# Expert pair 14's down products placed ahead of pair 15's gate products, with the last experts' gate and up matrices loaded in halves

## The chip, the cores and the metric

The kernel runs on one core of one Trainium2 chip. The metric is the device time of one launch in microseconds (us). The kernel before was timed in three runs: 791.98, 792.37 and 793.82 us, median 792.37 us.

## What is computed

One decoder layer: a mixer (a combined input projection, a convolution group, a state-space scan and an output projection) and then a mixture of 32 SwiGLU experts, of which each token uses two. The change touches only the experts. Cut to that part, the reference is:

```python
def hier_moe(h, ...):
    ...
    acc = jnp.zeros_like(t)
    for e in range(N_EXPERTS):
        hid = jax.nn.silu(t @ w_gate[e]) * (t @ w_up[e])
        acc = acc + combine[:, e:e + 1] * (hid @ w_down[e])
    return acc.reshape(shp)
...
    xp = xp + hier_moe(rmsnorm(xp, ln_ffn[l]), ...)
y_prompt = rmsnorm(xp, ln_final)
```

All is float32. There are 320 tokens of 1024 numbers. Each expert has three matrices (gate and up 1024 x 512, down 512 x 1024), 2048 KB each, so 96 matrices are read.

## The kernel before, in words

**Pairs of experts.** The experts are worked on in 16 pairs; pair i is experts 2i and 2i+1. Up to 64 tokens of each expert are gathered into 128 rows, 64 per expert. An expert's work on TensorE (PE) is made of these steps, all written out by hand in the order in which PE runs them:

- `tokens_T` (L1191, transposes at L1196): turns the gathered rows of a pair.
- `gate_up` (L1208, products at L1213 and L1214): the gate and the up product of one expert, side by side in the two halves of a bank. Each of the 8 steps over k reads one eighth of both matrices.
- ScalarE (ACT) then takes the silu of the gate half (`silu`, L1577, L1581), and VectorE (DVE) multiplies it with the up half (its loop at L2025, issued at L2029; the operation shows under the helper's line L1654).
- `hidden_T` (L1219, transposes at L1225): turns the pair's hidden rows when both experts have theirs; ACT copies them out of the bank (L1599).
- `expert_down` (L1250, products at L1236): the down product of one expert. It waits for that copy.
- `rows_back` (L1583, L1587) on ACT copies the two halves of a down product out of its bank.
- `combine_most` and `combine_rest` (L1274 and L1279, products at L1261): 10 and 2 products per pair that add the pair's rows onto the tokens' rows, which stay in five banks to the end. They wait for `rows_back` of both experts.

**Order on PE** (loop at L1287 to L1307). Pair i's stage is: gate of 2i; `combine_most` of pair i-2; gate of 2i+1; tokens of pair i+1; `combine_rest` of pair i-2; the two downs of pair i-1; `hidden_T` of pair i. So a pair's downs come a stage after its gates, and its combine two stages after. After the last stage come `combine_most` and `combine_rest` of pair 14, a register load of a token count (`value_load`, L1308), the down of expert 30, and the down of expert 31 in two halves (`down_half`, L1240, products at L1246), and the last combine with the closing norm.

**Order on ACT** (loop at L1591): for pair i the two silus, `rows_back` of both experts of pair i-1, and the copy of the hidden rows.

**Loads.** SyncE (SP) issues every matrix as one DMA, in the order in which PE reads them (`expert_units`, L61). The matrices live in 11 slots; matrix j takes the slot of matrix j-11, and SP waits until the product that read that one is done (L576 to L583), then issues (`load_expert`, L502, its DMA is L503). PE waits for a matrix in `expert_landed` (L427). Three early matrices (expert 1's down, expert 4's up, expert 5's gate) load in halves (`load_half`, L559, DMA at L561), and the first gate product has a wait in its middle (L1211) for the second half of its tokens.

**Banks.** The gate, token, down and hidden results take three banks in turn, in the order of `moe_jobs` (L181); `job_free` (L361) makes PE wait until the result three jobs ago has been read.

Of the kernel before, what the change touches and what calls it, by code (L numbers as in the profile page):

```python
# [47 lines left out]
NE, EG, NG = 32, 8, 4  # L48
# [7 lines left out]
UNIT = 4096  # L56
UNITS = ["ub0", "ua0", "ub1", "ua1", "x0", "x1", "x2", "z0", "z1", "o0", "o1", "o2", "o3"]
N_MIX = len(UNITS)


def expert_units():  # L61


    units = []
    for i in range(NE // 2):
        units += [(m, 2 * i + j) for j in range(2) for m in range(2)]
        if i:
            units += [(2, 2 * i - 2), (2, 2 * i - 1)]
    return units + [(2, NE - 2), (2, NE - 1)]


EXPERT = expert_units()
E_AT = {unit: j for j, unit in enumerate(EXPERT)}

# [106 lines left out]
def moe_jobs():  # L181

    tokens = lambda i: [("tokens", (i, h), "xgt", 2 * i + h + 1) for h in range(2)]
    down = lambda i: [("down", 2 * i + j, "yo", 2 * i + j + 1) for j in range(2)]
    jobs = tokens(0)
    for i in range(NE // 2):
        jobs += [("gate", 2 * i + j, "hid", 2 * i + j + 1) for j in range(2)]
        jobs += tokens(i + 1) if i + 1 < NE // 2 else []  # L190
        jobs += down(i - 1) if i else []
        jobs += [("hidden", i, "hidt", i + 1)]
    return jobs + down(NE // 2 - 1)

# [9 lines left out]
def build(nc, A, O):  # L204
    hn_dram = nc.dram_tensor("hn_scratch", (T, D), F32).ap()
    with ExitStack() as ctx:
# [5 lines left out]
        def S(name):  # L212
            if name not in sems:
                sems[name] = ctx.enter_context(nc.semaphore("s_" + name))
            return sems[name]
# [81 lines left out]

        h0 = [ring[:, (N_MIX + c // 4) % R, D * (c % 4):D * (c % 4) + D].rearrange("p (b n) -> p b n", b=NB)
              for c in range(NC)]
# [6 lines left out]
        xgt = zf[:, 0:D].rearrange("p (k s) -> p k s", k=KD)  # L306
# [3 lines left out]
        own_half = [slice(CAP * b, CAP * b + CAP) for b in range(2)]  # L310
# [28 lines left out]
        first = zf[:, 2048:2048 + 3 * P].rearrange("p (u s) -> p u s", u=3)  # L339
# [21 lines left out]
        def job_free(pe, kind, at):  # L361


            n = M[kind, at]
            if n >= 3:
                pe.wait_ge(S(MOE_JOBS[n - 3][2]), MOE_JOBS[n - 3][3])
            return bank[n % 3]
# [47 lines left out]
        def landed(eng, unit):  # L415
# [4 lines left out]

        mix_slot = [ring[:, (N_MIX + m) % R, :] for m in range(R)]
        e_slot = [xcx[:, 0:UNIT], mix_slot[2], mix_slot[0], mix_slot[3], rb[:, 0:UNIT], mix_slot[1], mix_slot[4],
                  mix_slot[5], ra[:, 0:UNIT], vy[:, D:D + UNIT], xv[:, 0:UNIT]]
        n_slot = len(e_slot)
        expert_in = [S(f"expert_in{s}") for s in range(n_slot)]

        def expert_landed(eng, m, e):  # L427


            j = E_AT[m, e]  # L430
            if j == n_slot - 2:
                eng.wait_ge(S("tenth_half"), 16)
            if j in (n_slot, n_slot + 1):
                eng.wait_ge(S("first_halves"), 32)
            eng.wait_ge(expert_in[j % n_slot], 16 * (j // n_slot + 1))
            return e_slot[j % n_slot]
# [14 lines left out]
        def _(sp_):  # L451
# [13 lines left out]
            def slot_free(n):  # L465

                if n >= R:
                    old = UNITS[n - R]
                    if old == "o3":
                        sp_.wait_ge(filled, J[("outs",)] + 1)  # L470
                    elif old[0] == "o":
                        sp_.wait_ge(S("wo_used"), int(old[1]) + 1)
                    else:
                        sp_.wait_ge(filled, J[last[old]] + 1)
# [27 lines left out]
            def load_expert(j):  # L502
                sp_.dma_start(e_slot[j % n_slot], expert_src(*EXPERT[j])).then_inc(expert_in[j % n_slot], 16)  # L503
# [5 lines left out]
            def load_states(half):  # L509
                slot_free(N_MIX + half)  # L510
                for c in range(4 * half, 4 * half + 4):
                    sp_.dma_start(h0[c], pair(A["state_ssm"], c)).then_inc(S(f"h0_in{half}"), 16)
# [22 lines left out]
            for c in range(NC):  # L535
                sp_.wait_ge(S("h0_new"), c + 1)
                sp_.dma_start(pair(O["new_ssm_sample"], c), h0[c]).then_inc(S(f"h0_out{c // 4}"), 16)
                if c == 1:
                    slot_free(N_MIX + 2)
                    load_expert(1)  # L540
# [3 lines left out]
                if c == 4:  # L544
                    slot_free(N_MIX + 3)
                    load_expert(3)
# [6 lines left out]
            for m in range(4, R):  # L553
                slot_free(N_MIX + m)
                load_expert(m + 2)
# [17 lines left out]
            sp_.wait_ge(S("gu_done"), 1)  # L573
            for j in (n_slot, n_slot + 1):
                load_half(j, 1, expert_in[j % n_slot])
            for j in range(n_slot + 2, len(EXPERT)):  # L576
                m, e = EXPERT[j - n_slot]

                if m < 2:
                    sp_.wait_ge(S("gu_done"), e + 1)  # L580
                else:
                    sp_.wait_ge(S("dn_done"), e + 1)
                load_expert(j)  # L583

            gain = A["ln_final"].rearrange("(a d) -> a d", a=1)
# [205 lines left out]
        def _(pe):  # L791
# [399 lines left out]
            def tokens_T(i, h):  # L1191


                to = job_free(pe, "tokens", (i, h))
                for k in range(4):
                    ins = pe.transpose(to[:, P * k:P * k + P], gat[:, 4 * h + k:D:KD], ident[:, :])  # L1196
                ins.then_inc(S("xg_T"), 1)
# [7 lines left out]

                pe.transpose(b_t[:, 0:P], ident[:, :], ident[:, :])

            def gate_up(to, x, wg, wu, first=False):  # L1208
                for k in range(KD):
                    st = dict(start=k == 0, stop=k == KD - 1)  # L1210
                    if first and k == 4:  # L1211
                        pe.wait_ge(S("xgt"), 2)
                    pe.matmul(to[0:CAP, :], x[:, k, :], wg[:, FE * k:FE * k + FE], **st)  # L1213
                    ins = pe.matmul(to[CAP:P, :], x[:, k, :], wu[:, FE * k:FE * k + FE], **st)  # L1214
                    if first and k == 3:
                        ins.then_inc(S("gu_half"), 1)
                return ins
# [56 lines left out]
            def combine_most(i):  # L1274
                pe.wait_ge(S("places"), i + 1)
                pe.wait_ge(S("yo"), 2 * i + 2)
                to_tokens(back[i % 2], yo_of, PARTS[:-1])

            def combine_rest(i):  # L1279
                to_tokens(back[i % 2], yo_of, PARTS[-1:]).then_inc(S("added"), 1)  # L1280
# [3 lines left out]
                tokens_T(0, h)  # L1284
            after_read(pe, "slots")

            for i in range(NE // 2):  # L1287
                for e in (2 * i, 2 * i + 1):
                    if i >= 2 and e % 2:
                        combine_most(i - 2)  # L1290
                    gate, up = expert_landed(pe, 0, e), expert_landed(pe, 1, e)
                    to = job_free(pe, "gate", e)
                    pe.wait_ge(S("xgt"), 2 * i + 2 if e else 1)
                    gate_up(to, xgt[:, :, own_half[e % 2]], gate, up, first=e == 0).then_inc(S("gu_done"), 1)
                more = i + 1 < NE // 2
                if more:
                    pe.wait_ge(S("gath"), 16 * (i + 2))
                    for h in range(2):
                        tokens_T(i + 1, h)
                if i >= 2:  # L1300
                    combine_rest(i - 2)
                if i:
                    expert_down(2 * i - 2)
                    expert_down(2 * i - 1)
                hidden_T(i)
            combine_most(NE // 2 - 2)
            combine_rest(NE // 2 - 2)  # L1307
            over = pe.value_load(mcount[0:1, 0:1], min_val=0, max_val=T)  # L1308
            expert_down(NE - 2)
            w_down = expert_landed(pe, 2, NE - 1)  # L1310
# [36 lines left out]
        def _(act):  # L1347
# [229 lines left out]
            def silu(e):  # L1577
                b = e % 2
                act.wait_ge(S("gu_done"), e + 1)
                wait(act, S("hid"), e - 1)  # L1580
                act.activation(sil[b], job_bank("gate", e)[0:CAP, :], ACT.Silu).then_inc(S("sil"), 1)  # L1581

            def rows_back(e):  # L1583
                act.wait_ge(S("dn_done"), e + 1)
                pt = job_bank("down", e)
                for q in range(2):
                    ins = act.activation(yo[own_half[e % 2], 512 * q:512 * q + 512],  # L1587
                                         pt[CAP * q:CAP * q + CAP, :], ACT.Copy)
                ins.then_inc(S("yo"), 1)

            for i in range(NE // 2):  # L1591
                silu(2 * i)
                silu(2 * i + 1)
                if i:
                    rows_back(2 * i - 2)
                    rows_back(2 * i - 1)
                act.wait_ge(S("hid_T"), i + 1)
                wait(act, S("dn_done"), 2 * i)
                act.activation(hidt, job_bank("hidden", i)[:, :].rearrange("p (k s) -> p k s", k=4), ACT.Copy)\  # L1599
                    .then_inc(S("hidt"), 1)  # L1600
# [521 lines left out]
```

## Time and profile before

| | us |
|---|---|
| three runs | 791.98, 792.37, 793.82 |
| median of the runs | 792.37 |
| the profiled execution, its span from the first to the last instruction | 789.4 |
| median less span (what lies around the span) | 2.97 |
| PE busy in the span | 757.8 (96%) |
| mean rate of the DMAs in the span | 316 GB/s |

A time of the profiled execution beside its span is not recorded apart, so its span is what sums are made against. In rows of the trace, PE is TensorE, SPq is the queue on which SP issues DMAs, and "issue" in the chain is time in which PE waited for nothing that the profile shows; a wait for a matrix that is still landing shows like that here. A group of rows shows "us from the span's start" first.

### The profile page before, as it was taken

Reading aid. Unit: us, or ns where it says so; the run is one execution under the profiler, and the core shown is the slowest. Engines: PE = TensorE matmul, PEld = TensorE weight load, DVE = VectorE, ACT = ScalarE, POOL = GpSimd, SP = SyncE. Lnnn points to the kernel's source line nnn. Section 1 sums busy time; section 2 is a strip of 40 time slices with the busy share of each in tenths; the row PEclk is TensorE's granted clock in tenths of the full one; section 3 lists DMA queues with packets and bytes.
Section 4 is the critical chain, followed back from the end, with each engine's and each line's share of the span. In section 5 each row is a group of like instructions: output and inputs, shape, how many; then the busy total and the mean of one; then the engine's idle time right before and its main releaser. Section 6 shows DMA issues by size and latency. Waiting matters only on the chain.

```text
span 789.4 us, 8694 instructions
## 1 busy us (share of the span) xinstructions
PE 757.8 (96%) x3470; PEld 360.5 (46%) x3470; DVE 270.5 (34%) x629; ACT 154.4 (20%) x308; POOL 140.3 (18%) x168
## 2 busy tenths in 40 slices
PE   6999999999999999799999999999999999989896
PEld 4667677767843335434333333333333333333332
DVE  2399499985656423511101101110110011011003
ACT  3211121245712003202011112101111110110122
POOL 2279998612002000100000000000000000000000
PEclk9999999999999999799999999999999999999998
DMA  9990610042659786999999999999999999999982
GB/s 312 304 364 10 230 40 1 9 107 108 188 213 275 252 306 237 368 374 414 429 426 427 425 429 425 425 430 426 427 427 426 425 426 427 427 429 425 429 356 69
DMA packets 51400, 249.58 MB, mean 316 GB/s; under 512 B 6982, under 2 KB 24422, under 8 KB 38671
## 3 DMA queue, kind: packets, MB, share of 16 engines
q1 hardware_dynamic: 45460, 243.40, 77.2%
q10 hardware_dynamic: 3371, 2.81, 1.2%
q0 software_dynamic: 2528, 2.79, 1.1%
q8 instruction: 29, 0.48, 0.2%
q14 instruction: 12, 0.10, 0.0%
HBM read 246.87 MB, written 8.61 MB: 324 GB/s over the span
## 4 chain that ended last, share of the span: by engine, by line
PE 91%; DMA 3%; DVE 2%; SPq 2%; issue 2%; ACT 1%; POOLq 0%; DVEq 0%
PE bank L1213 28%; PE bank L810 18%; PE bank L1236 14%; PE bank L1076 9%; PE bank L1261 9%; DMA xcx<-in_state_conf_conv 2%; PE bank L1196 2%; SPq L491 1%; PE bank L1225 1%; PE bank L1065 1%; PE bank L1034 1%; PE bank L905 1%; PE bank L1214 1%; PE bank L1122 1%; PE bank L1047 0%
## 5 line engine op out<-in xcount | busy, mean ns | idle before, releaser
L810 PE MATMUL bank<-region_a,ring 128*128 128x320 f32 x576 | 157.2, 433 | 1.0 <-DMA ring<-in_w_in 1.0
L1654 DVE TENSOR_TENSOR region_a<-region_a,bank 64x512 f32<-64x512 f32 (+1 forms) x33 | 22.5, 680 | 377.6 <-ACT region_a L1581 377.6
L1214 PE MATMUL bank<-ring,zz 128*64 128x512 f32 x320 | 145.4, 610 | 0.0
L1213 PE MATMUL bank<-ring,zz 128*64 128x512 f32 x288 | 127.3, 595 | 2.7 <-issue 2.7
L810 PEld LDWEIGHTS bank<-region_a,ring 128*128 128x128 f32 x576 | 108.7, 190 | 46.3 <-DVE region_a L1654 1.1
L1655 DVE SCALAR_TENSOR_TENSOR bank<-region_a,par,bank 128x256 f32<-128x256 f32 x232 | 91.2, 479 | 0.0
L763 POOL DMA_INDIRECT region_a<-hn_scratch,region_a x16 | 15.9, 996 | 369.6 <-PE bank L1196 355.8
L1261 PE MATMUL bank<-zz,masks 128*128 128x512 f32 (+1 forms) x192 | 77.2, 603 | 0.7 <-ACT zz L1587 0.7
L1213 PEld LDWEIGHTS bank<-ring,zz 128*64 128x64 f32 x288 | 38.1, 137 | 82.5 <-issue 81.7
L1076 PE MATMUL bank<-ring,x_v_y 128*128 128x512 f32 (+1 forms) x192 | 74.0, 605 | 0.0
L1581 ACT ACTIVATE region_a<-bank 64x512 f32<-64x512 f32 x32 | 18.9, 590 | 271.5 <-PE bank L1214 271.5
L1587 ACT ACTIVATE zz<-bank 64x512 f32<-64x512 f32 x60 | 35.5, 591 | 106.7 <-PE bank L1236 106.3
L1236 PE MATMUL bank<-ring,xcx 128*64 128x512 f32 x240 | 53.8, 596 | 0.0
L1076 PEld LDWEIGHTS bank<-ring,x_v_y 128*128 128x128 f32 (+1 forms) x192 | 26.7, 171 | 43.3 <-issue 43.0
L1261 PEld LDWEIGHTS bank<-zz,masks 128*128 128x128 f32 (+1 forms) x192 | 26.6, 172 | 39.1 <-issue 39.1
L1214 PEld LDWEIGHTS bank<-ring,zz 128*64 128x64 f32 x320 | 43.4, 140 | 0.0
L674 POOL TENSOR_TENSOR x_v_y<-x_v_y 128x512 f32<-128x512 f32 x29 | 36.8, 1270 | 2.3
L1213 PE MATMUL bank<-x_v_y,zz 128*64 128x512 f32 x80 | 35.4, 595 | 0.5 <-issue 0.5
L1236 PEld LDWEIGHTS bank<-ring,xcx 128*64 128x64 f32 x240 | 16.5, 137 | 35.8 <-issue 35.8
L1213 PE MATMUL bank<-xcx,zz 128*64 128x512 f32 x64 | 30.8, 638 | 2.0 <-issue 2.0
L672 POOL TENSOR_TENSOR x_v_y<-region_a,par 128x512 f32<-128x512 f32 x30 | 32.2, 1074 | 2.2
L1214 PE MATMUL bank<-x_v_y,zz 128*64 128x512 f32 x64 | 28.3, 595 | 0.0
(313 smaller groups left out, 770.1 us busy)
## 6 DMA issues: line engine op xcount, KB each, us to landing
ring<-in_expert_w_up SPq DMA_DIRECT2D x20, 2048.0 KB, 24.4
ring<-in_expert_w_gate SPq DMA_DIRECT2D x17, 2048.0 KB, 30.3
ring<-in_expert_w_down SPq DMA_DIRECT2D x16, 2048.0 KB, 34.8
ring<-in_w_in SPq DMA_DIRECT2D x9, 2048.0 KB, 15.7
x_v_y<-in_expert_w_down SPq DMA_DIRECT2D x6, 2048.0 KB, 33.5
x_v_y<-in_expert_w_gate SPq DMA_DIRECT2D x5, 2048.0 KB, 34.6
ring<-in_w_out SPq DMA_DIRECT2D x4, 2048.0 KB, 10.0
xcx<-in_expert_w_gate SPq DMA_DIRECT2D x4, 2048.0 KB, 31.8
```

The costliest lines, as they stand in the source:

```text
L672: link(pool.tensor_tensor(tmp4, u_seq[:, :, :, k:k + TB], w4(par, k, NC), ALU.mult))
L674: return link(pool.tensor_tensor(acc, acc, tmp4, ALU.add))
L810: ins = pe.matmul(pt[0:m, 0:T], w[:, k, :], ht[:, k, :], start=k == 0, stop=k == KD - 1)
L1076: return pe.matmul(dst, mix, w, start=c == 0, stop=c == 2 * NC - 1)
L1213: pe.matmul(to[0:CAP, :], x[:, k, :], wg[:, FE * k:FE * k + FE], **st)
L1214: ins = pe.matmul(to[CAP:P, :], x[:, k, :], wu[:, FE * k:FE * k + FE], **st)
L1236: ins = pe.matmul(to[CAP * q:CAP * q + CAP, :], x[:, k, :], wd[:, D * k + 512 * q:D * k + 512 * q + 512], start=k == 0, stop=k == 3)
L1261: return pe.matmul(dst, rows[:, t0:t0 + n], of[q][0:rows.shape[0], :], start=False, stop=end)
L1581: act.activation(sil[b], job_bank("gate", e)[0:CAP, :], ACT.Silu).then_inc(S("sil"), 1)
L1587: ins = act.activation(yo[own_half[e % 2], 512 * q:512 * q + 512], pt[CAP * q:CAP * q + CAP, :], ACT.Copy)
L1654: tt_ = lambda out, a, b, op: dve.tensor_tensor(out, a, b, op)
L1655: stt = lambda out, a, s_, b, op0, op1: dve.scalar_tensor_tensor(out=out, in0=a, scalar=s_, in1=b, op0=op0, op1=op1)
```

## The change

Three things are done, all for the last pairs:

- The order on PE, on ACT, of the banks and of the matrices changes for pair 15: the downs of pair 14 come ahead of the gates of pair 15. PE now runs, after stage 14: the whole combine of pair 13, the downs of experts 28 and 29, the whole combine of pair 14, the gates of experts 30 and 31, `hidden_T` of pair 15, the register load, and the downs of 30 and 31 as before.
- ACT copies the down rows of experts 28 and 29 out ahead of the silus of 30 and 31.
- The gate and up matrices of experts 30 and 31 load in two halves each, in the order first half of gate, first half of up, second half of gate, second half of up. PE starts a gate product with the first halves and waits in its middle (k = 4) for the second.

```diff
--- before.py
+++ after.py
@@ -56,6 +56,7 @@
 UNIT = 4096
 UNITS = ["ub0", "ua0", "ub1", "ua1", "x0", "x1", "x2", "z0", "z1", "o0", "o1", "o2", "o3"]
 N_MIX = len(UNITS)
+LAST = NE // 2 - 1
 
 
 def expert_units():
@@ -63,9 +64,9 @@
 
     units = []
     for i in range(NE // 2):
-        units += [(m, 2 * i + j) for j in range(2) for m in range(2)]
-        if i:
-            units += [(2, 2 * i - 2), (2, 2 * i - 1)]
+        downs = [(2, 2 * i - 2), (2, 2 * i - 1)] if i else []
+        gates = [(m, 2 * i + j) for j in range(2) for m in range(2)]
+        units += downs + gates if i == LAST else gates + downs
     return units + [(2, NE - 2), (2, NE - 1)]
 
 
@@ -186,9 +187,10 @@
     down = lambda i: [("down", 2 * i + j, "yo", 2 * i + j + 1) for j in range(2)]
     jobs = tokens(0)
     for i in range(NE // 2):
+        jobs += down(i - 1) if i == LAST else []
         jobs += [("gate", 2 * i + j, "hid", 2 * i + j + 1) for j in range(2)]
-        jobs += tokens(i + 1) if i + 1 < NE // 2 else []
-        jobs += down(i - 1) if i else []
+        jobs += tokens(i + 1) if i < LAST else []
+        jobs += down(i - 1) if 0 < i < LAST else []
         jobs += [("hidden", i, "hidt", i + 1)]
     return jobs + down(NE // 2 - 1)
 
@@ -573,13 +575,22 @@
             sp_.wait_ge(S("gu_done"), 1)
             for j in (n_slot, n_slot + 1):
                 load_half(j, 1, expert_in[j % n_slot])
-            for j in range(n_slot + 2, len(EXPERT)):
+            def place_free(j):
                 m, e = EXPERT[j - n_slot]
-
-                if m < 2:
-                    sp_.wait_ge(S("gu_done"), e + 1)
-                else:
-                    sp_.wait_ge(S("dn_done"), e + 1)
+                sp_.wait_ge(S("gu_done") if m < 2 else S("dn_done"), e + 1)
+
+            for j in range(n_slot + 2, E_AT[0, NE - 2]):
+                place_free(j)
+                load_expert(j)
+            for e in (NE - 2, NE - 1):
+                pair_of = (E_AT[0, e], E_AT[1, e])
+                for j in pair_of:
+                    place_free(j)
+                    load_half(j, 0, S(f"late_half{e % 2}"))
+                for j in pair_of:
+                    load_half(j, 1, expert_in[j % n_slot])
+            for j in range(E_AT[2, NE - 2], len(EXPERT)):
+                place_free(j)
                 load_expert(j)
 
             gain = A["ln_final"].rearrange("(a d) -> a d", a=1)
@@ -1205,11 +1216,14 @@
 
                 pe.transpose(b_t[:, 0:P], ident[:, :], ident[:, :])
 
-            def gate_up(to, x, wg, wu, first=False):
+            def gate_up(to, x, wg, wu, first=False, late=None):
                 for k in range(KD):
                     st = dict(start=k == 0, stop=k == KD - 1)
                     if first and k == 4:
                         pe.wait_ge(S("xgt"), 2)
+                    if late is not None and k == 4:
+                        expert_landed(pe, 0, late)
+                        expert_landed(pe, 1, late)
                     pe.matmul(to[0:CAP, :], x[:, k, :], wg[:, FE * k:FE * k + FE], **st)
                     ins = pe.matmul(to[CAP:P, :], x[:, k, :], wu[:, FE * k:FE * k + FE], **st)
                     if first and k == 3:
@@ -1284,7 +1298,7 @@
                 tokens_T(0, h)
             after_read(pe, "slots")
 
-            for i in range(NE // 2):
+            for i in range(LAST):
                 for e in (2 * i, 2 * i + 1):
                     if i >= 2 and e % 2:
                         combine_most(i - 2)
@@ -1292,19 +1306,30 @@
                     to = job_free(pe, "gate", e)
                     pe.wait_ge(S("xgt"), 2 * i + 2 if e else 1)
                     gate_up(to, xgt[:, :, own_half[e % 2]], gate, up, first=e == 0).then_inc(S("gu_done"), 1)
-                more = i + 1 < NE // 2
-                if more:
-                    pe.wait_ge(S("gath"), 16 * (i + 2))
-                    for h in range(2):
-                        tokens_T(i + 1, h)
+                pe.wait_ge(S("gath"), 16 * (i + 2))
+                for h in range(2):
+                    tokens_T(i + 1, h)
                 if i >= 2:
                     combine_rest(i - 2)
                 if i:
                     expert_down(2 * i - 2)
                     expert_down(2 * i - 1)
                 hidden_T(i)
-            combine_most(NE // 2 - 2)
-            combine_rest(NE // 2 - 2)
+            combine_most(LAST - 2)
+            combine_rest(LAST - 2)
+            expert_down(NE - 4)
+            expert_down(NE - 3)
+            combine_most(LAST - 1)
+            combine_rest(LAST - 1)
+            for e in (NE - 2, NE - 1):
+
+
+                pe.wait_ge(S(f"late_half{e % 2}"), 32)
+                gate, up = (e_slot[E_AT[m, e] % n_slot] for m in range(2))
+                to = job_free(pe, "gate", e)
+                pe.wait_ge(S("xgt"), 2 * LAST + 2)
+                gate_up(to, xgt[:, :, own_half[e % 2]], gate, up, late=e).then_inc(S("gu_done"), 1)
+            hidden_T(LAST)
             over = pe.value_load(mcount[0:1, 0:1], min_val=0, max_val=T)
             expert_down(NE - 2)
             w_down = expert_landed(pe, 2, NE - 1)
@@ -1589,9 +1614,12 @@
                 ins.then_inc(S("yo"), 1)
 
             for i in range(NE // 2):
+                if i == LAST:
+                    rows_back(2 * i - 2)
+                    rows_back(2 * i - 1)
                 silu(2 * i)
                 silu(2 * i + 1)
-                if i:
+                if 0 < i < LAST:
                     rows_back(2 * i - 2)
                     rows_back(2 * i - 1)
                 act.wait_ge(S("hid_T"), i + 1)
```

## Rows read from the trace of the kernel before

**Rows 1.** The page's GB/s in 40 slices of the span.

```profile
GB/s 312 304 364 10 230 40 1 9 107 108 188 213 275 252 306 237 368 374 414 429 426 427 425 429 425 425 430 426 427 427 426 425 426 427 427 429 425 429 356 69
```

**Rows 2.** Chain of work that ended last, from 705 us: start, us, what.

```profile
705.67 2.69 issue
...
728.05 7.02 PE bank L1236 x32
735.07 0.68 PE bank L1225 x4
735.75 1.99 issue
...
746.42 3.63 PE bank L1261 x10
...
757.07 1.06 PE bank L1261 x2
758.13 7.04 PE bank L1236 x32
...
766.53 4.71 PE bank L1261 x12
771.24 3.58 PE bank L1236 x16
774.83 3.45 PE bank L1246 x32
```

**Rows 3.** SP's timeline: the issue of expert 30's up matrix.

```profile
696.07 0.33 SPq L503 DMA_DIRECT2D ring<-in_expert_w_up  x1
```

**Rows 4.** DMA issues of 696.0 to 696.3 us: KB, us from issue to landing.

```profile
ring<-in_expert_w_up SPq DMA_DIRECT2D x1, 2048.0 KB, 41.6
```

**Rows 5.** Line L503: down matrices into the ring; first and last start.

```profile
L503 SPq DMA_DIRECT2D ring<-in_expert_w_down x16: 327/328/3068, 348.2 to 726.1; - x16
```

**Rows 6.** DMA issues of 726 to 727 us: the last matrix, expert 31's down.

```profile
ring<-in_expert_w_down SPq DMA_DIRECT2D x1, 2048.0 KB, 41.3
```

**Rows 7.** Timeline of ACT after 757 us: silu, rows back, hidden copy, table load.

```profile
757.12 0.59 ACT L1581 ACTIVATE region_a<-bank 64x512 f32<-64x512 f32 x1 [10.07 <-PE bank L1214]
...
765.19 1.19 ACT L1587 ACTIVATE zz<-bank 64x512 f32<-64x512 f32 x2 [2.24 <-PE bank L1236]
766.41 0.60 ACT L1599 ACTIVATE xcx<-bank 128x512 f32<-128x512 f32 x1
767.02 1.28 ACT L1611 ACT_TABLE_LOAD   x1
```

**Rows 8.** Timeline of DVE: the product after the last silu.

```profile
757.74 0.69 DVE L1654 TENSOR_TENSOR region_a<-region_a,bank 64x512 f32<-64x512 f32 x1 [9.90 <-ACT region_a L1581]
```

**Rows 9.** SP's timeline near 341 us: second halves of two early matrices.

```profile
340.98 0.33 SPq L561 DMA_DIRECT2D xcx<-in_expert_w_up  x1
341.35 0.43 SPq L561 DMA_DIRECT2D ring<-in_expert_w_gate  x1
```

**Rows 10.** DMA issues of 341.3 to 341.6 us: those two halves, us to landing.

```profile
xcx<-in_expert_w_up SPq DMA_DIRECT2D x1, 1024.0 KB, 7.8
ring<-in_expert_w_gate SPq DMA_DIRECT2D x1, 1024.0 KB, 9.9
```

**Rows 11.** PE's timeline in the first gate product, about its middle.

```profile
336.90 0.59 PE L1213 MATMUL bank<-xcx,zz 128*64 128x512 f32 x1
337.33 0.59 PE L1213 MATMUL bank<-xcx,zz 128*64 128x512 f32 x1
```

**Rows 12.** PE's timeline: start of expert 24's gate product.

```profile
648.75 1.00 PE L1213 MATMUL bank<-region_b,zz 128*64 128x512 f32 x1 [1.90 <-issue]
```

**Rows 13.** Stretches: busy PE, PEld, DVE, ACT, POOL; then PEclk, DMA share, GB/s.

```profile
650.00:654.00 4.00, 4.00 (x16) 1.48 (x14) 0.00 (x0) 0.00 (x0) 0.00 (x0) 0.72 1.05 442
...
708.00:710.00 2.00, 1.64 (x8) 0.74 (x10) 0.00 (x0) 0.00 (x0) 0.00 (x0) 1.00 0.96 410
...
738.00:740.00 2.00, 2.00 (x6) 0.55 (x5) 0.00 (x0) 0.00 (x0) 0.00 (x0) 0.50 0.98 418
```

## The prediction

> **What bounds the kernel now.** I read the page's rates first. From about 340 us to 765 us the DMAs move 425 to 430 GB/s without a break, and only the last two slices fall off [rows 1]: in the expert stage the stream of matrices runs flat out. The chain of waits then shows how PE stands to that stream. PE is busy almost throughout, but at the start of a pair it waits for a matrix: 2.69 us ahead of expert 28's gate product and 1.99 us ahead of expert 30's [rows 2]. That these are landings is seen from SP: expert 30's up matrix was issued at 696.07 us [rows 3] and landed 41.6 us later [rows 4], at 737.67; the gate product starts at 735.75 + 1.99 = 737.74. The last matrix, expert 31's down, was issued at 726.1 [rows 5] and landed 41.3 us later [rows 6], at 767.4. Between the two landings lie six matrices, so one takes (767.4 - 737.67)/6 = 4.95 us. PE starts expert 31's down only at 774.83 [rows 2], 7.4 us after its landing. So up to 737.7 us the stream sets the pace, and from there PE alone does. What the end costs is PE's own work from there, and every hole in it.
>
> **What the change removes.** The next matrices in line become the downs of 28 and 29. They take the places that expert 30's gate and up had, so they land at 732.7 and 737.7, and PE has other work until then. The wait of 1.99 us is gone. A second loss goes with it. The gate product behind that wait took 746.42 - 737.74 = 8.68 us, expert 31's only 757.07 - 750.05 = 7.02 us (750.05 is the end of the ten combine products, 746.42 + 3.63) [rows 2]. The cause is the clock: granted clock 0.50 from 738 to 740 us [rows 13], which is the 1.2 GHz level. A fall thus costs 1.66 us. Both together are 3.65 us.
>
> **What it adds: PE's new order, step by step.** I start at 735.07, where the downs of 26 and 27 end and the transposes of pair 14's hidden rows begin [rows 2]; up to there nothing changes, since the order of the matrices is the same up to expert 27's down.
>
> 1. The combine of pair 13 needs the rows of expert 27 copied back. The same step stands in the trace one pair on: downs end at 758.13 + 7.04 = 765.17, ACT copies for 1.19 us [rows 7], the combine starts at 766.53 [rows 2]. That is 1.36 us, with the transposes inside it. So the combine starts at 736.43 and takes 4.71 as pair 14's does [rows 2]: 741.14.
> 2. Downs of 28 and 29, 7.04 us [rows 2]: 748.18. Their matrices have landed, and the hidden rows of pair 14 were copied long before.
> 3. Again 1.36 us until the rows of 29 are back: 749.54. Before, the transposes of pair 15 filled half of this hole; now nothing does.
> 4. Combine of pair 14, 4.71: 754.25.
> 5. Gates of 30 and 31, 7.02 each: 768.29.
> 6. Now the pair's hidden chain stands bare. Before, it lay behind the combine and the downs of pair 14. Its parts: gate end to product end 758.43 - 757.07 = 1.36 (silu, then DVE's product) [rows 7, 8]; transposes 0.68 [rows 2]; ACT's copy 0.60 [rows 7]; the three hand-overs between PE and ACT or DVE, 0.03, 0.05 and, as from ACT's copy to the combine, 766.53 - 766.38 = 0.15. Together 2.87: the down of 30 starts at 771.16.
>
> Before, it starts at 771.24 [rows 2]. From there on all is as before. **The sum is -0.08 us.** What is saved, 1.99 + 1.66, is given back as a bare hidden chain (2.87) and as longer holes at the two copies back.
>
> **What costs nothing, and what covers it.** The halves are eight DMAs of 1 MB in place of four of 2 MB, so four more issues on SP of 0.33 to 0.43 us each [rows 9], 1.7 us at most, while SP issues some 41 us ahead of a landing [rows 4, 6]. Two second halves in the trace were issued at 340.98 and 341.35 [rows 9] and landed 7.8 and 9.9 us later [rows 10], at 348.78 and 351.25: 2.47 us apart, half of a whole matrix's 4.95. So I take no loss of rate. Expert 31's second halves land at about 757.5; the product's middle is at 761.27 + 3.5 = 764.8. The cover is 7.3 us there, and as much for the last down (767.4 against 774.7). If it were gone, each us over it would be paid in full. The mid-product wait: in the first gate product, which has one, its ninth pair starts 0.43 us after its eighth [rows 11], the pace of the others, so a satisfied wait is free; the other end, from the same rows, is one lost pair per gate, 0.86 us in all, and I take 0. The register load on PE used to sit behind twelve combine products; now it sits behind four transposes, with 0.60 us of ACT's copy over it. On ACT the same load and its branch leave no gap: the copy ends at 767.01, the table load starts at 767.02 [rows 7], so it fits. Bound: 0 to 0.6, I take 0. SP's later waits (the final gain, the last downs) ask for the same products as before, and these end no later.
>
> The Trainium skill's page DMA: Bandwidth & Descriptors (Anatomy of one DMA — SWDGE (gpsimd) path) gives about 2 us of fixed cost for each DMA, on a path other than SP's. By it, as an estimate, four more would make the stream 8 us late, 0.7 us more than its cover; the landings 2.47 us apart speak against that here.
>
> **The unknown: the clock in the new stall.** A fall of the clock is the term that decides. The trace has three waits of such a length. After 1.90 us ahead of expert 24's gate [rows 12] the clock was 0.72 in the next stretch [rows 13]; after 1.99 us it was 0.50; after 2.69 us it stayed at 1.00 [rows 2, 13]. So two of three. The new hidden chain keeps PE from products for 2.87 us (2.19 us idle, the rest transposes), like those. I take a fall there as more likely than not, at 1.66 us, all on the path, since only downs and the last combine follow. A second place: a fall behind the 2.69 us wait did not happen in this execution. Before the change the wait of 1.99 us would have swallowed it; now nothing would, and it would be worth another 1.66. The three runs lie 1.84 us apart, about one fall, so I expect it to differ from run to run.
>
> **Forecast**, chance 0.40: one fall after the change, where the profiled execution had one: -0.08 + 1.66 = +1.58 us, 789.4 + 1.58 = 790.98 of span. The span lies 2.97 us under the median of the runs, which I leave as it is: 792.37 + 1.58, about 794.0 us.
>
> **Rivals.**
>
> - *No fall in the new stall* (0.22). For it: one of three stalls, and the transposes break it. Time 792.37 - 0.08 = 792.3. The Trainium skill's page TensorE: Matmul & The Clock Gate (Why this matters for your kernels) blames longer idle gaps than these for the clock's return to the low level; by it this rival would hold, but the fall after 1.90 us speaks against it.
> - *One fall more than that* (0.27): both places, or one place against runs of before that had none. For it: in two of three stalls the clock fell. +3.24: 795.6.
> - *Faster: the stream is the brake* (0.08). Before the change PE waits for expert 30's matrices in full; after it, it has 7 us in hand. If the six matrices up to there took 5.2 us each instead of 4.9 (735.75 + 1.99 less 705.67 + 2.69 is 29.4 for six), the old wait would be 1.8 us longer and the change worth -1.9: 790.5. It decides from 5.15 us on. Against it: 4.90 and 4.95 in two stretches of the trace.
> - *Halves do harm* (0.03): a fixed cost for each DMA, or SP's issues blocked. It needs over 7 us to show; at 8 us it gives +0.7, 793.1 without a fall and 794.7 with one.
>
> **How the numbers follow.** About 0.2%, 1.58 us, is what a measurement of this kernel can tell from no change; the forecast sits on that line. Slower by more: the 0.27, a little over half of the forecast's 0.40, and part of the last rival, 0.52. Same: the 0.22 and the rest of the forecast, 0.40. Faster: 0.08. The range goes from 791.2 (no fall, and a stream 1 us slower) to 796.0 (two falls and 0.4 of the bounds); it leaves out the faster rival and three falls.
>
> **What would show it.** In the profile after: no wait ahead of expert 30's gate; the combine of pair 13 some 1.4 us behind the downs of 27; a second such hole behind 29's; about 2.9 us between the last gate product and the first down product of 30, and the downs of 30 starting near 771 us where no fall preceded. The halves show as eight issues of 1024 KB, none of them waited for. Right on the clock is a granted clock of 0.50 behind the last gates. Wrong: a wait inside gates 30 or 31 (halves late), a hidden chain much shorter or longer than 2.9 us, or downs of 30 that start well before 770 us, for which I have no step.

## The result, and the profile after

The change made the kernel slower: 796.42 us median of 20 runs (793.46 to 799.0) against 793.5 us of the kernel before, also in 20 runs (790.55 to 797.9). The ratio is 1.0033, 95% interval 1.0018 to 1.0047, or 2.6 us of 793.5. It is not the quotient of the two medians, which lie 2.92 us apart. The direction and the larger share of the chances were right; the time of 794.0 us was too low, and 796.42 lies 0.4 us above the range.

The span of the profiled execution is 792.1 us, against 789.4. With the result each run's span stands beside its time: the two are 1.66 to 1.90 us apart in every run, not 2.97. So, as an estimate, the profiled execution before was a run of some 791.2 us, 2.3 us under the median of 20; the one after took 793.83 us, 2.6 us under its own. Both lie under their medians by about as much, so they can be set against each other.

The chain of waits after the change (start, us, what) answers to [rows 2]; first the wait ahead of expert 28's gate, then all from the downs of experts 26 and 27 on:

```profile
708.54 0.95 issue
...
729.17 7.04 PE bank L1250 x32
...
736.84 0.60 ACT zz L1612
737.44 0.14 issue
737.58 4.71 PE bank L1275 x12
742.28 7.04 PE bank L1250 x32
...
749.95 0.60 ACT zz L1612
750.55 0.14 issue
750.69 4.71 PE bank L1275 x12
755.39 0.57 PE bank L1227
...
768.85 0.42 PE bank L1227
...
769.33 0.60 ACT region_a L1606
...
769.95 0.70 DVE region_a L1682
770.65 0.14 issue
770.79 0.73 PE bank L1239 x4
...
771.54 0.61 ACT xcx L1627
772.15 0.09 issue
772.24 5.35 PE bank L1250 x16
777.59 3.45 PE bank L1260 x32
```

L1250 is a down product, L1275 the combine, L1227 a gate product, L1239 the transposes. The order is the predicted one. The downs of 26 and 27 end at 736.21, the combine of pair 13 starts 1.37 us later (1.36 was said), the second such hole is 1.37 us too, the two gates end at 769.30, and the hidden chain stands bare for 2.94 us (2.87 was said). From the end of those downs to the down of 30 it is 772.24 - 736.21 = 36.03 us; the prediction had 36.09, and the kernel before 36.17 [rows 2]. So in this stretch nothing was won.

What the profile lost lies at two other places. Expert 30's down took 5.35 us where the old one took 3.58 [rows 2]: 1.77 us for a fall of the clock. The stretches (busy PE, PEld, DVE, ACT, POOL; then granted clock, DMA share, GB/s) show it, beside the earlier fall that this execution had behind its wait of 3.09 us at the start of pair 13:

```profile
680.00:684.00 4.00, 4.00 (x14) 1.46 (x12) 0.00 (x0) 0.00 (x0) 0.00 (x0) 0.57 1.02 430
...
772.00:776.00 4.00, 3.76 (x10) 1.42 (x12) 0.00 (x0) 1.63 (x3) 0.00 (x0) 0.57 0.02 4
```

And the stretch began 1.14 us later (736.21 against 735.07), which no part of the change explains, since order and loads are the same up to there. It is there at the start of expert 26's gate already, 679.47 us against 678.30. Together -0.14 + 1.77 + 1.14 = 2.77, and the spans differ by 2.7.

Another distance is of use below. The last wait for a matrix in the change is the one of 0.95 us ahead of expert 28's gate, which starts at 709.49 us. From there on PE alone sets the pace, and the down of 30 follows 772.24 - 709.49 = 62.75 us later. In the kernel before it is 771.24 - 708.36 = 62.88 us, with a fall of the clock inside [rows 2].

The halves were on time but their issue was not as cheap as said. Part of SP's timeline (start, us, what; x2 is two issues with the time between them) and the landing of expert 31's last half (KB, us to landing):

```profile
708.11 6.75 SPq L563 DMA_DIRECT2D ring<-in_expert_w_up  x1
714.90 4.25 SPq L563 DMA_DIRECT2D region_b<-in_expert_w_gate  x1
719.20 4.23 SPq L563 DMA_DIRECT2D ring<-in_expert_w_up  x1
723.47 4.49 SPq L563 DMA_DIRECT2D region_b<-in_expert_w_gate  x1
728.00 4.24 SPq L563 DMA_DIRECT2D ring<-in_expert_w_up  x1
732.29 6.39 SPq L505 DMA_DIRECT2D ring<-in_expert_w_down  x2
```

```profile
ring<-in_expert_w_up SPq DMA_DIRECT2D x1, 1024.0 KB, 31.2
```

SP stood 4.2 us and more in each of these five issues of halves, not 0.33 to 0.43. PE did not wait for it: the last half landed at 728.0 + 31.2 = 759.2, and PE reached the middle of that product some 3.5 us ahead of its end at 769.30, at 765.8.

### The profile page after: what moved, and what is told of

It is laid out like the page before. It is cut to its first block, busy times and chain, and to the rows that moved or that the text cites. A ratio compares the mean times of both kernels' runs of the same rounds, so it can differ in the third digit from the quotient of the medians.

```text
span 792.1 us, 8698 instructions
## 1 busy us (share of the span) xinstructions
PE 761.2 (96%) x3470; PEld 362.9 (46%) x3470; DVE 272.7 (34%) x629; ACT 154.5 (20%) x308; POOL 140.2 (18%) x168
## 4 chain that ended last, share of the span: by engine, by line
PE 73%; DVE 5%; issue 2%; ACT 1%; DMA 0%; DVEq 0%; POOLq 0%
PE bank L1227 28%; PE bank L1250 14%; PE bank L1087 9%; PE bank L1275 9%; PE bank L1207 2%; PE bank L1239 1%; DVE bank L1683 1%; PE bank L821 1%; PE bank L1076 1%; PE bank L1045 1%; PE bank L916 1%; PE bank L1228 1%; DVE x_v_y L1683 1%; DVE bank L1721 1%; PE bank L1133 1%
## 5 line engine op out<-in xcount | busy, mean ns | idle before, releaser
L1228 PE MATMUL bank<-ring,zz 128*64 128x512 f32 x320 | 142.1, 599 | 0.0
L1227 PE MATMUL bank<-ring,zz 128*64 128x512 f32 x288 | 127.3, 595 | 0.9 <-issue 0.9
L1275 PE MATMUL bank<-zz,masks 128*128 128x512 f32 (+1 forms) x192 | 76.9, 602 | 2.1 <-ACT zz L1612 2.1
L1227 PEld LDWEIGHTS bank<-ring,zz 128*64 128x64 f32 x288 | 38.1, 137 | 80.7 <-issue 80.0
L1250 PE MATMUL bank<-ring,xcx 128*64 128x512 f32 x240 | 55.5, 611 | 0.7 <-ACT xcx L1627 0.7
L1275 PEld LDWEIGHTS bank<-zz,masks 128*128 128x128 f32 (+1 forms) x192 | 26.6, 172 | 40.4 <-issue 40.4
L1227 PE MATMUL bank<-x_v_y,zz 128*64 128x512 f32 x80 | 37.1, 618 | 3.1 <-issue 3.1
L1250 PEld LDWEIGHTS bank<-ring,xcx 128*64 128x64 f32 x240 | 17.2, 140 | 36.9 <-issue 36.9
L1227 PE MATMUL bank<-region_b,zz 128*64 128x512 f32 x64 | 28.2, 594 | 2.3 <-issue 1.7
L1228 PE MATMUL bank<-x_v_y,zz 128*64 128x512 f32 x64 | 28.3, 595 | 0.0
```

Of the source, the lines that this page charges most:

```text
L1250: ins = pe.matmul(to[CAP * q:CAP * q + CAP, :], x[:, k, :], wd[:, D * k + 512 * q:D * k + 512 * q + 512], start=k == 0, stop=k == 3)
L1275: return pe.matmul(dst, rows[:, t0:t0 + n], of[q][0:rows.shape[0], :], start=False, stop=end)
```

## The experiments

Every kernel was timed in 12 runs, beside 22 to 35 runs of the kernel before on the same chip. One interval is 0.0014 to 0.0022 wide on either side, some 1.1 to 1.7 us, so single microseconds are seen only as a pattern over several kernels, or as distances within the traces. The quotient of two medians differs from the ratio given by up to 0.0011.

### The two halves of the change apart

**The order alone.** The matrices of 30 and 31 load whole:

```diff
-            for j in range(n_slot + 2, E_AT[0, NE - 2]):
...
+            for j in range(n_slot + 2, len(EXPERT)):
                 place_free(j)
                 load_expert(j)
...
-                pe.wait_ge(S(f"late_half{e % 2}"), 32)
-                gate, up = (e_slot[E_AT[m, e] % n_slot] for m in range(2))
+                gate, up = expert_landed(pe, 0, e), expert_landed(pe, 1, e)
```

> The change's order without its halves: the gate and up matrices of experts 30 and 31 load whole. Theory (the bare hidden chain, the longer holes at the copies back and the clock's falls cost the time; the halves do nothing): same as the change, 1.0033 of before within about 0.0015, and in the profile no wait ahead of expert 30's gate, some 2.9 us between expert 31's last gate product and expert 30's first down product. Rival (the halves hold up the stream or SP): back to 0.999 to 1.001 of before, with matrices landing earlier than in the change's profile.

Measured: 795.97 us, ratio 1.0029 (1.0015 to 1.0043). No wait ahead of expert 30's gate. Its chain behind the last gate product:

```profile
773.88 0.60 ACT region_a L1593
...
775.20 0.14 issue
775.33 0.74 PE bank L1229 x4
...
776.70 0.09 issue
776.79 3.65 PE bank L1240 x16
```

The same bare chain, and here the clock did not fall: it was granted at 1.00 from 774 to 780 us, and the down took 3.65 us. From the start of expert 28's gate to the down of 30 it is 776.79 - 714.04 = 62.75 us, as in the change. So the order is what costs; a help or harm from the halves does not show within the intervals.

**The halves alone**, in the old order: SP and `gate_up` as in the change, the loops of PE, ACT and the banks as before.

```diff
-                    gate, up = expert_landed(pe, 0, e), expert_landed(pe, 1, e)
+                    late = e if e >= 30 else None
+                    if late is None:
+                        gate, up = expert_landed(pe, 0, e), expert_landed(pe, 1, e)
+                    else:
+                        pe.wait_ge(S(f"late_half{e}"), 32)
+                        gate, up = (e_slot[E_AT[m, e] % n_slot] for m in range(2))
...
```

> The old order with the change's halves: the gate and up matrices of experts 30 and 31 load in halves, PE starts with the first ones. Theory: expert 30's gate starts without its wait of about 2 us, since its first halves have landed at about 732.8 us of the old profile and the second ones land within the product; nothing is laid bare. Start of the down of 30 some 2.0 us earlier, and 1.7 us more in executions whose clock fell behind that wait: 0.9960 to 0.9980 of before. Rival (halves do harm): 1.000 or more, with a wait in the middle of a gate product.

Measured: 791.4 us, ratio 0.998 (0.9963 to 0.9996): faster than before. PE's timeline at expert 30's gate, and at the down of 29:

```profile
736.15 0.75 PE L1241 MATMUL bank<-ident,region_a 128*128 128x128 f32 x4
736.82 0.64 PE L1229 MATMUL bank<-xcx,zz 128*64 128x512 f32 x1
```

```profile
760.23 3.65 PE L1252 MATMUL bank<-ring,xcx 128*64 128x512 f32 x16 [1.03 <-DMA ring<-in_expert_w_down]
```

The gate starts right behind the transposes: the wait of 1.99 us [rows 2] is gone, and nothing was moved for it. Half of that comes back: PE now waits 1.03 us for the down of 29, which is the stream's next landing. So the halves took the old wait away by themselves, at the upper edge of the expected range, and the reordering spent more than that.

### The clock

**A first try, mis-sized.** The change with full-width products in the new stall, whose results nobody reads:

```diff
+            def warm(to, n):
+                for _ in range(n):
+                    pe.matmul(to[:, :].rearrange("p (a e) -> p a e", e=P), ident[:, :],
+                              bc(ident[:, :].unsqueeze(1), [P, 4, P]), start=True, stop=True)
...
+            warm(job_free(pe, "hidden", LAST), 3)
             hidden_T(LAST)
+            warm(job_free(pe, "down", NE - 2), 1)
```

> The change with three products whose results nobody reads ahead of the last transposes of hidden rows and one behind them, so that PE runs products while it waits for the hidden chain. The chain itself is as long as before. Theory (a fall of the clock in that stall is part of the loss): no granted clock of 0.50 on expert 30's down, which takes 3.6 us and not 5.35; the time lies 0.9 to 1.5 us under the change's: 1.0015 to 1.0022 of before. Rival (only the stall's length costs, the clock falls elsewhere as often): 1.0033 as the change.

Measured: 796.31 us, ratio 1.0037 (1.002 to 1.0053). The filling was too long. Each product shows as two of 0.46 us:

```profile
769.75 2.77 PE bank L1244 x6
...
773.85 3.58 PE bank L1255 x16
```

The stall grew from 2.94 to 4.10 us, by 1.16. That the ratio hardly rose hints that something was saved against it, but it settles nothing.

**The same with half-width products** (`to[:, 0:2 * P]`, 256 columns):

> The change with products whose results nobody reads in the new stall, this time half as wide (256 columns, 0.43 us each): three ahead of the last transposes, one behind them, 1.72 us in all, so that they fit into the stall of 2.97 us. Theory (falls of the clock in that stall are part of the loss): the down of 30 still starts about 2.97 us behind the last gate product, takes 3.58 us in every profile and no granted clock of 0.50 lies on it; time 1.0018 to 1.0026 of before. Rival (the clock's falls cost nothing on the mean): 1.0033.

Measured: 794.27 us, ratio 1.0017 (0.9998 to 1.0036).

```profile
770.60 1.49 PE bank L1244 x6
...
772.11 0.73 PE bank L1239 x4
...
772.86 0.60 ACT xcx L1634
773.47 0.09 issue
773.56 3.65 PE bank L1255 x16
```

The stall keeps its length, 773.56 - 770.60 = 2.96 us, and the down takes 3.65 us. The granted clock is 1.00 from 770 to 778 us. The ratio is 0.0016 under the change's, 1.3 us; the medians, each against the kernel before beside it, give 2.4. That is the size that theory wants for falls of the clock in the new stall, but the two intervals overlap, so it is not shown by this pair alone.

**Both kernels without falls.** The same filling also in the waits at the start of pairs 12 to 14 of the change, and of pairs 12 to 15 of the kernel before:

```diff
+                    if e in (24, 26, 28):
+                        warm(job_free(pe, "gate", e), 3)
                     gate, up = expert_landed(pe, 0, e), expert_landed(pe, 1, e)
```

> The change with such narrow products in the new stall and also three of them (1.29 us) in the waits at the start of pairs 12, 13 and 14, so that no fall of the clock is left from there to the end. Theory: what is left over before is the longer holes alone, -0.08 + 1.66 = 1.6 us against a kernel before without falls, so this kernel lies 0.0020 over the kernel before with the same filling; and about 0.0010 to 0.0020 under the change. Rival (falls do not count): 1.0033, as the change.

> The kernel before with three such narrow products in the waits at the start of pairs 12 to 15. Theory: the falls behind the first three waits were swallowed by the next wait anyway, only the one behind the last wait counted, in less than half of the runs: 0.9985 to 0.9996 of before. Granted clock 1.00 from 640 us to the end. Rival (the old kernel lost as much to the clock as the new one): 0.9965 to 0.9980.

Measured: the change 794.26 us, ratio 1.0013 (0.9991 to 1.0035); the kernel before 793.42 us, ratio 1.0 (0.9981 to 1.0018). In both profiles the granted clock is 1.00 in all stretches from 640 us to 780 us. They differ by 0.0013, 1.0 us, where the holes alone were to make 1.6; the intervals take in that and zero. The traces agree with the smaller number: from the start of expert 28's gate to the down of 30 it is 772.54 - 709.79 = 62.75 us in the change and 774.26 - 712.27 = 61.99 in the kernel before, 0.76 apart. There PE stood 742.35 - 739.66 = 2.69 us between the transposes and expert 30's gate, filling and wait together, where the first profile had 1.99. The kernel before gained nothing measurable from the filling: its own falls were worth less than was thought, though the interval leaves room for up to 1.5 us. With its stall filled, the change lies at 1.0017 and 1.0013; without, at 1.0033, and at 1.0029 without the halves. That is a pattern, and no more.

### The holes

**The combine of pair 14 between the gates.** It covers the hole behind 29's downs and leaves the hidden chain bare:

```diff
-            combine_most(LAST - 1)
-            combine_rest(LAST - 1)
             for e in (NE - 2, NE - 1):
+                if e % 2:
+                    combine_most(LAST - 1)
+                    combine_rest(LAST - 1)
```

> The change with the combine of pair 14 between the gates of experts 30 and 31. The hole of 1.32 us behind 29's downs is covered by expert 30's gate; the hidden chain stays bare, 2.97 us, and with it the falls of the clock there. Theory (both holes count, each by its own length): 1.3 us under the change, 1.0010 to 1.0022 of before. Rival (the bare hidden chain with its falls is all of the loss): 1.0030 or more.

Measured: 793.29 us, ratio 0.9995 (0.9976 to 1.0015). This is 3.0 us under the change, more than the hole of 1.32 to 1.37 us; only the lower part of the expected range lies inside the interval. The rival falls. In the trace it is 774.82 - 712.29 = 62.53 us from the start of expert 28's gate to the down of 30, and that gate took 8.48 us behind a wait of 2.83, 1.40 more than the 7.08 it takes without a fall. Less that it is 61.13, 1.6 under the change's 62.75, about the hole. The bare chain brought no fall here (the down took 3.65 us).

**The combine about the transposes**, so that it covers the hidden chain as well:

```diff
-            combine_most(LAST - 1)
-            combine_rest(LAST - 1)
             for e in (NE - 2, NE - 1):
...
+            combine_most(LAST - 1)
             hidden_T(LAST)
+            combine_rest(LAST - 1)
```

> The change with the combine of pair 14 moved behind the gates: its ten products between expert 31's gate and the transposes, its two behind them. This takes away the hole behind 29's downs and covers the hidden chain. Theory (the holes are the loss): the down of 30 starts 3.6 us earlier than in the change (by the old rows: 767.6 us against 771.2), and no fall of the clock there: 0.9960 to 0.9985 of before, 0.0050 under the change. Rival (halves, or the stream, hold PE up): PE meets waits inside the gates of 30 and 31 and little is gained, 1.001 or more.

> The kernel with the combine of pair 14 about the last transposes once more, on the chip of the run with the filled waits: 0.9945 to 0.9980 of before.

Measured: 789.93 us, ratio 0.9962 (0.9943 to 0.9982), and on another chip 791.16 us, 0.9976 (0.9955 to 0.9997): faster than both kernels, both times. The chain of the first, from the end of the gates:

```profile
765.31 3.63 PE bank L1275 x10
768.94 0.47 PE bank L1239 x4
769.41 0.86 PE bank L1275 x2
770.27 3.58 PE bank L1250 x16
```

There is no hole left between the last gate product and the down of 30. The distance from expert 28's gate is best read from the profile on the other chip, in which the granted clock is 1.00 from 690 to 780 us:

```profile
712.12 0.95 issue
713.08 0.61 PE bank L1227
...
771.58 3.58 PE bank L1250 x16
```

It is 771.58 - 713.08 = 58.50 us, 4.25 less than in the change and in the order alone, and 3.49 less than in the kernel before with its waits filled. With the order and the halves of the change kept and only this one step put elsewhere, loss turns into gain. That settles that the bare chain and the hole were the loss; how much the falls that come with them added is not settled.

**The same without falls behind the stream's waits**, filled as above:

> The kernel with the combine of pair 14 about the last transposes, with three narrow products whose results nobody reads in the waits at the start of pairs 12, 13 and 14. With the holes covered, no wait for the stream follows pair 14's start, so theory says a fall of the clock behind that wait is paid in full at the end: without it 0.3 to 1.2 us less than the kernel with the combine alone on the same chip, and expert 28's gate takes 7.1 us in every profile. Rival (falls behind that wait are made up later): the same as it.

Measured: 789.73 us, ratio 0.9962 (0.9941 to 0.9983), 1.1 us under the unfilled kernel beside it. The difference has the expected size but is within the noise. That such a fall is paid when it comes is seen in the two profiles of the unfilled kernel. In the first, behind a wait of 2.82 us, the clock was at 0.50, and expert 28's gate took 718.86 - 708.89 = 9.97 us, where it takes 7.1 otherwise. The down of 30 then came 770.27 - 708.89 = 61.38 us after the start of that gate, against 58.50 in the second, without the fall: 2.88 us, all of it carried to the end.

```profile
708.89 1.09 PE L1227 MATMUL bank<-ring,zz 128*64 128x512 f32 x1 [2.82 <-issue]
```

```profile
708.00:712.00 4.00, 3.11 (x8) 1.11 (x10) 0.00 (x0) 0.00 (x0) 0.00 (x0) 0.50 0.98 418
...
712.00:716.00 4.00, 4.00 (x14) 1.25 (x12) 0.00 (x0) 0.00 (x0) 0.00 (x0) 0.66 1.03 434
```

### How far the halves go

**Halves for the last two pairs in the old order** (experts 28 to 31; `e >= 28` in the edit above, and SP likewise), and **halves for two pairs with the combine about the transposes**:

> The old order with the gate and up matrices of the last two pairs (experts 28 to 31) in halves. Theory (PE has the holes of its own order alone to lose, and the stream's landing of a whole matrix at a pair's start): the wait ahead of expert 28's gate goes too, 2.7 us more than with the last pair alone, of which a wait of about 1 us in expert 30's gate and one ahead of expert 29's down come back: 0.9945 to 0.9970 of before. Rival (the stream ends the kernel): as the halves of the last pair alone, 0.9980.

> The kernel with the combine of pair 14 about the last transposes, and the gate and up matrices of experts 28 and 29 in halves as well. Theory: the wait ahead of expert 28's gate, 2 to 3 us, goes; the stream then holds PE inside expert 31's gate for up to 1.3 us: 1.4 to 2.7 us under the kernel with the combine alone, 0.9930 to 0.9950 of before. Rival (the stream's last landings end the kernel already): 0.9962, with waits for the downs of 30 and 31.

Measured: 790.56 us, 0.9962 (0.9944 to 0.998), and 791.13 us, 0.997 (0.9953 to 0.9988). The first lies in its range and is about as fast as the combine about the transposes with halves for one pair. In its trace the wait ahead of expert 28's gate is gone, and waits of 1.34 us in the middle of expert 30's gate, 0.60 in that of 31's and 1.25 ahead of the down of 29 come instead, for matrices that are still landing. The second gains nothing that can be told from noise: 0.997 against 0.9976 for halves of one pair on the same chip. By the time its rival is nearer than its theory, but the waits for the downs of 30 and 31 that the rival names are not there. PE's timeline in it:

```profile
762.50 0.61 PE L1231 MATMUL bank<-region_b,zz 128*64 128x512 f32 x1 [0.49 <-DMA ring<-in_expert_w_up]
```

PE waits inside expert 31's gate for the second halves, 0.49 us, so the stream holds PE there once more. In this profile there was little to win ahead of it: the clock fell behind a wait of 3.53 us at expert 26's gate (granted 0.63 from 684 to 688 us), and expert 28's gate starts 711.90 - 682.89 = 29.01 us after it, against 30.02 in the change.

## Why the prediction was wrong, point by point

- **The bound, and that the wait of 1.99 us would go: right.** No wait ahead of expert 30's gate in any kernel with the new order. That the old wait was worth taking away is shown by the halves alone (0.998). Its size differs from execution to execution: 2.69 us with the filled waits. The rates were read a little wide: 425 GB/s and more stand in the slices from 375 to 750 us, not from 340 to 765 [rows 1].
- **PE's new order, step by step: right.** 36.03 us in the profile after against 36.09 in the sum; the two holes 1.37 us each against 1.36, the hidden chain 2.94 against 2.87.
- **A fall in the new stall, 1.66 us, more likely than not: open.** It took 1.77 us in the profile after. Of the three profiles with the bare chain and nothing in it, one has the fall; the order alone and the combine between the gates have none. The filled kernel puts it at 1.3 us on the mean, within the noise. That the one profile of the change has it is in part luck.
- **The step that failed in the base: "The span lies 2.97 us under the median of the runs, which I leave as it is".** The median of three runs, 792.37, is 1.13 us under the median of 20, 793.5. A forecast of +1.58 on the latter is 795.1, and the range would have reached 797.1. Of the miss of 2.4 us, 1.1 are this and 1.3 lie in the sum; the base alone puts the result outside the range. The 2.97 us are not what lies around the span, either: that is 1.66 to 1.90 us, and the rest is that the profiled execution lay under the median.
- **What the three runs were taken to show.** They differed by 1.84 us, which was read as one fall; the 20 differ by 7.35. A good part of that arises ahead of the change: the first transposes of tokens, at the head of the experts, start at 330.99 us in the profile before and 331.26 in the one after, but at 335.15 in the order alone, behind a wait of 5.41 us for the gathered rows, and at 334.79 in the kernel before with its waits filled.
- **The step that failed in the sum: "Both together are 3.65 us".** The 1.66 us in it, the fall behind the old wait, was netted as saved because the profiled execution had it. When it comes, it is paid: from the start of expert 30's gate to the end it is 789.4 - 737.74 = 51.7 us in the profile before and 792.4 - 742.35 = 50.1 with the waits filled. But the runs show no saving on the mean: the kernel before with its waits filled is at 1.0 (0.9981 to 1.0018). Without that credit the prediction's own terms give +1.58 for the holes less the old wait and +1.66 for the fall, 3.24 us, which is its rival of one fall more; on the median of 20 that is 796.7, against 796.42 measured. The interval leaves room for part of the credit, and the profiles with filled waits put the holes less the old wait at 0.76 us and not 1.58, so how the measured 2.6 to 2.9 us divide between holes and falls stays open.
- **Halves cost nothing: right in effect** (order alone 1.0029, with halves 1.0033). The fixed cost of each DMA that the Trainium skill gives (DMA: Bandwidth & Descriptors, Anatomy of one DMA — SWDGE (gpsimd) path) did not add up on SP's path: the last half landed at 759.2 us, 1.7 later than forecast in an execution that was 1.14 us late already, and 6.6 us ahead of its use. "1.7 us at most" of SP's time was wrong, 4.2 us and more for one issue, but covered. The rows that the prediction shows had an issue of 3.07 us in them [rows 5].
- **The rivals.** "One fall more" at +3.24 stood on the side that came; the result lies between it and the forecast. One of its two places, behind the wait ahead of expert 28's gate, is seen in two of the seven profiles with the new order in which that wait was left as it is, and there it is paid in full, up to 2.88 us. "No fall" holds in single executions only. "The stream is the brake" did not come: the change has no wait for a matrix behind 709.5 us, though six matrices took 709.49 - 679.47 = 30.0 us there, 5.0 each and not 4.90.

## What to carry to other kernels

A step that is moved takes its cover along: before pulling work forward out of the end of a kernel, ask which chain of dependent steps on other engines ran behind it, and leave the longest piece of independent work there. A cheap remedy at the place of the wait (halves of the two matrices that PE waits for) can do what a reordering is meant to do, without laying anything bare; here half of the wait came back at the next matrix. And of a stall that one profile shows together with its clock, credit only the stall: whether the clock falls differs from run to run, and three runs are too few to fix a median when single runs lie 7 us apart.

## What the runs showed that I had not expected

- The length of a wait alone does not tell whether the clock falls behind it. It stayed at full rate behind waits of 2.75 and 2.66 us in the profile of the order alone:

```profile
681.25 2.75 issue
683.99 0.61 PE bank L1217
...
711.38 2.66 issue
714.04 0.61 PE bank L1217
```

and the granted clock is 1.00 from 680 to 692 us and from 712 to 724. It fell behind 2.82 us in another kernel and 1.99 us in the one before. In all profiles with unfilled waits at the start of pairs 12 to 15, waits of 1.90 to 2.75 us were followed by a fall seven times and by none seven times. The same bare chain brought a fall in one kernel and none in two others.

- SP stood inside the issue of one half for 4.2 to 6.8 us, at a time when the last half landed 31.2 us after its issue. Most of the same kernel's earlier issues, and those near 341 us before [rows 9], took 0.33 to 0.43. What the longer ones wait for is not shown; in the kernel before, too, one took 3.07 us [rows 5]. It delayed no landing that PE waited for.
